# Group norm of the y tiles inside a two-direction scan: elementwise steps moved from VectorE and ScalarE to GpSimd

## The reference, cut to what matters

```python
_, ys = lax.scan(step, S0, xs)
y = (ys[:, 0] + ys[::-1, 1]).transpose(1, 0, 2, 3)       # two directions summed, (B, T, H, N)
mu = jnp.mean(y, axis=-1, keepdims=True)
var = jnp.mean(jnp.square(y - mu), axis=-1, keepdims=True)
y = ((y - mu) * lax.rsqrt(var + LNX_EPS)).reshape(B, T, C)
y = (y * lnx_g + lnx_b)                                   # then bonus, gate, output projection
```

## Time and profile before

| | value |
|---|---|
| runs | 1659.62 us median of 3 (1654.68 to 1660.95) |
| profiled execution | 1656.46 us, span 1654.7 us |
| TensorE busy in the span | 1476.4 us (89%) |
| VectorE busy | 791.2 us (48%) |
| ScalarE busy | 462.9 us (28%) |
| GpSimd busy | 46.0 us (3%) |
| mean granted TensorE clock | 0.944 |

### The profile page before, as it was taken

One profiled execution on the slowest core, in us unless ns is written; L12 is line 12 of the kernel. 1 busy time (PEld: TensorE's weight loads), 2 busy tenths in 40 slices (PEclk: granted clock), 3 DMA queues, 4 the chain that ended last, 5 costly groups with the idle time before them and its releaser, 6 DMA issues.

```text
span 1654.7 us, 27385 instructions
## 1 busy us (share of the span) xinstructions
PE 1476.4 (89%) x11156; PEld 1088.5 (66%) x11156; DVE 791.2 (48%) x985; ACT 462.9 (28%) x685; POOL 46.0 (3%) x45
## 2 busy tenths in 40 slices
PE   7889899899299998973995999999999999999993
PEld 3354544544177777762883888888788888788882
DVE  5656284678066777777237333322233321233335
ACT  3414243100034555553122333211122210122221
POOL 0100010101100000002000000000000000000000
PEclk9999999999688999886997999999999999999997
DMA  5045737463655565521110111111111111111112
GB/s 190 29 114 118 171 86 165 106 157 89 198 175 155 145 201 163 181 68 58 64 40 23 51 40 49 51 51 51 38 51 51 43 46 51 40 50 51 38 38 101
DMA packets 153463, 148.40 MB, mean 90 GB/s; under 512 B 75120, under 2 KB 130544, under 8 KB 153296
## 3 DMA queue, kind: packets, MB, share of 16 engines
q1 hardware_dynamic: 149136, 136.48, 28.7%
q0 software_dynamic: 1728, 5.64, 1.2%
q10 hardware_dynamic: 2560, 5.77, 1.1%
HBM read 106.04 MB, written 41.81 MB: 89 GB/s over the span
## 4 chain that ended last, share of the span: by engine, by line
PE 78%; DVE 12%; ACT 3%; issue 3%; DMA 2%; SPq 1%; DVEq 0%; ACTq 0%
PE banks L490 48%; PE banks L478 16%; PE banks L655 2%; PE banks L645 1%; PE banks L687 1%; PE banks L672 1%; PE banks L615 1%; PE banks L626 1%; DVE hT L1070 1%; PE banks L560 1%; PE banks L605 1%; PE banks L696 1%; PE banks L497 1%; DVE bonusT L1067 1%; DVE h_lo L1051 1%
## 5 line engine op out<-in xcount | busy, mean ns | idle before, releaser
L490 PE MATMUL banks<-h_hi,w_hi 128*128 128x512 f32 x832 | 259.3, 393 | 27.4 <-DVE h_lo L1051 14.3
L478 PE MATMUL banks<-hT,work 128*128 128x512 f32 x576 | 255.0, 603 | 18.4 <-DVE hT L1113 6.4
L490 PE MATMUL banks<-h_lo,w_hi 128*128 128x512 f32 x832 | 257.9, 391 | 0.0
L490 PE MATMUL banks<-h_hi,w_lo 128*128 128x512 f32 x832 | 257.6, 391 | 0.0
L478 PEld LDWEIGHTS banks<-hT,work 128*128 128x128 f32 x576 | 110.5, 193 | 160.0 <-issue 146.6
L490 PEld LDWEIGHTS banks<-h_hi,w_hi 128*128 128x128 f32 x832 | 156.7, 189 | 64.7 <-issue 27.9
L938 ACT ACTIVATE w_hi<-work 128x1024 fp32r<-128x1024 f32 x76 | 80.2, 1057 | 383.7 <-PE banks L490 383.7
L490 PEld LDWEIGHTS banks<-h_lo,w_hi 128*128 128x128 f32 x832 | 157.3, 189 | 33.2
L490 PEld LDWEIGHTS banks<-h_hi,w_lo 128*128 128x128 f32 x832 | 157.3, 189 | 33.0
L1341 DVE TENSOR_TENSOR xT<-xT,banks 128x1024 f32<-128x1024 f32 (+1 forms) x32 | 39.1, 1221 | 239.8 <-PE banks L490 239.8
L490 PE MATMUL banks<-g_hi,w_lo 128*128 128x512 f32 x352 | 108.4, 389 | 0.0
(11 more groups left out here) (161 smaller groups left out, 1748.1 us busy)
## 6 DMA issues: line engine op xcount, KB each, us to landing
work<-scan_d SPq DMA_DIRECT2D x32, 768.0 KB, 4.7
work<-in_w_gu SPq DMA_DIRECT2D x44, 512.0 KB, 3.5
scan_d<-work SPq DMA_DIRECT2D x16, 1024.0 KB, 6.0
work<-in_w_in SPq DMA_DIRECT2D x20, 512.0 KB, 3.9
scan_d<-work SPq DMA_DIRECT2D x32, 256.0 KB, 6.2
work<-in_w_down SPq DMA_DIRECT2D x16, 512.0 KB, 3.6
work<-v_d SPq DMA_DIRECT2D x64, 64.0 KB, 4.5
xT<-in_xT POOLq DMA_DIRECT2D x8, 512.0 KB, 7.8
```

The costliest lines, as they stand in the source:

```text
L478: mm = pe.matmul(out[:, h * HALF:(h + 1) * HALF], wt[:, k, :], src[:, k, h * HALF:(h + 1) * HALF], start=(k == 0), stop=(k == kn - 1))
L490: mm = pe.matmul(out[:, h * HALF:(h + 1) * HALF], wp[slot][:, k, :], xp[:, k, h * HALF:(h + 1) * HALF], start=(k == 0 and p_ == 0), stop=( ...
```

## The change

In the late passes, GpSimd now adds the two directions, subtracts the mean, squares (as a product of the centred tile with itself) and multiplies by the inverse deviation. VectorE keeps the sum over heads with its scaling (`y_mean`, at the places of `y_centre`), both variance sums (now both in q = 3) and the reciprocal (`y_inverse`, at the place of `y_normalise`). ScalarE keeps the square root and no longer squares in the scan. The tail's two tiles are done as before, behind a new wait for GpSimd's last product.

```diff
--- before.py
+++ after.py
@@ -921,8 +921,6 @@
 
                                 act.wait_ge(ys_stored[q % 2], 64 * (2 * i + q // 2) + FREE)
                             act.activation(Ys[q % 2][:, z], banks[:, z, 0:256], ACT.Copy).then_inc(sz[z]["Y_out"], 1)
-                        if late and q in (1, 2):
-                            y_square(2 * i + (q - 1 - 2 * YT), q - 1)
             exponentials(2 * (NC // 4) - 1, 1, (3,))
             transposed(2 * (NC // 4) - 1)
             attended(NC // 4 - 1, 1)
@@ -1035,6 +1033,28 @@
                 pool.dma_start(xT[:, k, :], a["xT"][:, k, :]).then_inc(s["x_again"], 16)
 
 
+            heads = lambda x: x.rearrange("p (h n) -> p h n", n=HD)
+            by_head = lambda x: x.rearrange("p (e j) c -> p j e c", e=2)
+            with pool.Fori(YT, NC // 4) as i:
+                for slot in range(2):
+                    r = i + (1 - YT)
+                    pool.wait_ge(y_full[slot], 16 * r)
+                    pool.tensor_tensor(ysum[slot], yin[slot][:, 0], yin[slot][:, 1], ALU.add).then_inc(yin_used[slot], 1)
+                for slot in range(2):
+                    m = 2 * i + (slot - 2 * YT)
+                    pool.wait_ge(s["y_chain"], 2 * m + 2)
+                    pool.tensor_tensor(heads(ycen[slot]), heads(ysum[slot]),
+                                       stat[slot][:, 0].unsqueeze(2).broadcast_to([P, AH, HD]), ALU.subtract)\
+                        .then_inc(s["y_cent"], 1)
+                    pool.wait_ge(s["y_cent"], m + 1)
+                    pool.tensor_tensor(ysq[slot], ycen[slot], ycen[slot], ALU.mult).then_inc(s["y_sq"], 1)
+                for slot, tile in ((0, i * -1 + NC // 4), (1, i + -1)):
+                    pool.wait_ge(s["y_inv"], 2 * i + (slot - 2 * YT) + 1)
+                    pool.tensor_tensor(yn[:, :, bass.ds(tile, 1), :].rearrange("p j o (e c) -> p j (o e) c", e=2),
+                                       by_head(heads(ycen[slot])),
+                                       by_head(stat[slot][:, 3].unsqueeze(2).broadcast_to([P, AH, HD])), ALU.mult)\
+                        .then_inc(s["y_normed"], 1)
+
             for k in range(NPAIR, KD):
                 pool.wait_ge(sp_s["att_hi"], k - NPAIR + 1)
                 pool.tensor_tensor(h_lo[:, k, :], oT[:, k, :], h_hi[:, k, :].bitcast(F32), ALU.subtract)\
@@ -1248,6 +1268,18 @@
 
             heads = lambda x: x.rearrange("p (h n) -> p h n", n=HD)
 
+            def y_mean(m, r, slot):
+
+                dve.wait_ge(yin_used[slot], r + FREE)
+                dve.tensor_reduce(stat[slot][:, 0], heads(ysum[slot]), AX.X, ALU.add).then_inc(s["y_chain"], 1)
+                dve.wait_ge(s["y_chain"], 2 * m + 1)
+                ts(stat[slot][:, 0], stat[slot][:, 0], 1.0 / HD, None, ALU.mult).then_inc(s["y_chain"], 1)
+
+            def y_inverse(m, slot):
+
+                dve.wait_ge(s["y_sd"], m + 1)
+                dve.reciprocal(stat[slot][:, 3], stat[slot][:, 2]).then_inc(s["y_inv"], 1)
+
             def y_centre(m, r, slot):
 
                 dve.wait_ge(y_full[slot], 16 * r)
@@ -1294,9 +1326,8 @@
                         if cc == 0:
                             dve.wait_ge(s["p_exp"], 8 * i + 4 * g + FREE)
                             logits(i, g, (0, 1, 2, 3))
-                        if late and q == 2:
+                        if late and q == 3:
                             y_variance(2 * i - 2 * YT, 0)
-                        elif late and q == 3:
                             y_variance(2 * i + (1 - 2 * YT), 1)
                         for z in range(2):
                             c = n if z == 0 else (i * -4 + (NC - 1 - q))
@@ -1307,12 +1338,13 @@
                             tt(S[:, z], St[:, z], PC[:, z, :, bass.ds(c, 1)].broadcast_to([P, NPAIR, HD]), ALU.mult)\
                                 .then_inc(sz[z]["S_new"], 1)
                         if late and q in (1, 2):
-                            y_centre(2 * i + (q - 1 - 2 * YT), i + (1 - YT), q - 1)
+                            y_mean(2 * i + (q - 1 - 2 * YT), i + (1 - YT), q - 1)
                         elif late and q == 3:
-                            y_normalise(2 * i - 2 * YT, i * -1 + NC // 4, 0)
-                            y_normalise(2 * i + (1 - 2 * YT), i + -1, 1)
+                            y_inverse(2 * i - 2 * YT, 0)
+                            y_inverse(2 * i + (1 - 2 * YT), 1)
 
             normalise(2 * (NC // 4) - 1, 1)
+            dve.wait_ge(s["y_normed"], NT - 2 + FREE)
             for slot in range(2):
                 y_centre(NT - 2 + slot, NT // 2, slot)
             for slot in range(2):
```

## The result

The changed kernel takes 1649.96 us, the one before 1658.83 us beside it (medians of 14 runs each). The ratio is 0.9948, 95% interval 0.9929 to 0.9967: 8.9 us faster, and clear of no change. The forecast was 1651.3 us, 8.3 us less.

What follows compares the result with a forecast made beforehand. TensorE holds 78% of the chain of waits, so VectorE savings count only where TensorE waits. Savings of 1.23 + 1.53 = 2.76 us in each of three late passes make 8.3: 1659.62 - 8.3 = 1651.3 us, range 1645 to 1660.

Steps and rivals of the forecast that it cites:

- q = 3: Late pass, end of q = 2 to TensorE's next L645: ScalarE no longer squares, saving 1.53 us.
- The bound: TensorE holds 78% of the chain; group norm's 18 us in three late passes are all the change can touch in the scan.
- q = 2: Late pass, between the ends of VectorE's last state products: 9.71 us instead of 10.94, saving 1.23 us.
- the two products: End of q = 3, the two L1273 moved to GpSimd: beside TensorE's wait for the Y copies, so worth nothing.
- g, GpSimd's instruction: Duration of one GpSimd instruction on a 128x512 tile: taken as 1.09 us, kept between 1.0 and 2.16.
- the slower rival: Long GpSimd instructions delay VectorE in q = 2 and q = 3: with 2.16 us each, 1664.2 us; chance 0.15.
- The add's cover: End of q = 1: GpSimd's add is over by about 674.5, `y_mean` comes at 676.2, 1.7 us in hand.
- if L1307 is stretched in q = 1: Sign that the prediction would be wrong: VectorE's state product in q = 1 takes longer; no size given.
- The clock rival: TensorE's clock in q = 0 moves: 3 us less, 1648.3, or as much more, 1654.3; chance 0.1 each.

Runs made afterwards that it cites:

- square twice: The changed kernel with each square done twice on GpSimd, first into a spare tile: 1650.20 us, ratio 0.9944.
- the held-back one: The changed kernel with GpSimd's subtraction and square of slot 0 held back until VectorE's L1266 of q = 2 is done: 1647.03 us, ratio 0.9926.

## Why the prediction was right

- **The bound.** That only the scan's late passes could gain, and there only q = 2 and q = 3, holds: 8.65 us of the profile lie there. Putting back what was costed at nothing (the two products) changed nothing; putting back what was costed (the squares) did.
- **g, GpSimd's instruction.** Taken 1.09 us, measured 1.04 for subtraction and square, 1.06 for the product and 1.27 for the add. The broadcast operand, which gave the slower rival its case, costs nothing: the subtraction has one, the square none.
- **q = 2.** Forecast 9.71, measured 9.21, so 1.73 us saved instead of 1.23. The order is the one forecast (L1262 slips in or waits, the square goes first, L1266 waits for it), with L1266 at 2.47 against "about 2.6". Its terms were a little long, all four in the same direction: the hand-over from VectorE to GpSimd, 0.08 us instead of 0.23; that between GpSimd's two instructions, 0.08 instead of 0.2; the two instructions themselves, 0.10 together; and the start of VectorE's product, of which some 0.15 us pass while it waits (L1266 ends 1.62 us after the square, and takes 1.76 where nothing is in its way).
- **q = 3.** Forecast 8.24, measured 8.18, 1.59 us saved instead of 1.53. L1252 was stretched by 0.08 instead of 0.4, within the slack. Both variance sums end in time. The edit with the squares on ScalarE shows that 1.27 us of this saving are ScalarE's. That holds for passes 5 and 6. The third pass has no L645 behind it; from the end of its q = 2 to the tail's first add it took 24.91 us before and 23.32 after, which is 1.59 less as well, but 23.32 with the squares back on ScalarE too, and 21.89 with the subtraction held back. Whether q = 3 earned the third 1.59 isn't shown.
- **The add's cover.** `y_mean` doesn't wait for it, as forecast. But the prediction looked only at that wait and missed the other side: in pass 5, the y load lands later and the add runs into the first state product, 1.18 us instead of 0.43. q = 1 takes 8.05 instead of 7.30. It had named "if L1307 is stretched in q = 1" as what would make it wrong, and this step of it was, by 0.75 us once. These two rows are VectorE's and GpSimd's of the changed kernel:

```profile
647.87 1.18 DVE L1338 TENSOR_TENSOR work<-work,PC 128x256 f32<-128x256 f32 x1
```

```profile
646.16 2.60 POOL L1042 TENSOR_TENSOR work<-work 128x512 f32<-128x512 f32 x2 [189.28 <-DMA work<-y_d]
```

- **The slower rival.** Its mechanism holds for a longer instruction, but its price was too high: "4 us a pass for each us of g". With the square alone longer by 0.85 us, half of that rule is 1.7; the pass grew by 0.85 + 0.42 = 1.27, as q = 3 has more slack than was counted. In the changed kernel ScalarE starts its exponentials 0.49 us after the negated maxima are there (pass 6), where the prediction had the maxima 0.06 us late.
- **The clock rival** is real but goes both ways: q = 0 took 12.03 and 9.10 us in the changed kernel, 10.49 and 10.48 before, the sum nearly the same.

The sum therefore closes: three times 1.73 + 1.59 is 9.96, minus 0.75 for pass 5; the remaining difference to 8.65 is q = 0 and q = 1 of the single passes (1.54 and 0.41 lost, 1.38 gained). That the total came so near to the forecast 8.3 is in part luck. The two places gave 1.7 us more than forecast, and q = 1, at which nothing was forecast, took 1.16 back. And the clock moved single q = 0 pieces by 1.5 us between these two kernels and by up to 4.4 between all, so a forecast that is right to 0.6 us is closer than its mechanism can vouch for.

## What to carry to other kernels

An engine that is 28% busy can be the one that holds up the step: look for what its next instruction waits for, not for its load. When elementwise work goes to GpSimd, find VectorE's products with two SBUF inputs (and its small operations of one input, like the negated maxima) and keep GpSimd's reads away from them by one wait, or at least keep GpSimd's instructions short: in these traces VectorE got in between two of them and never into one that reads. And before hiding a table switch in a loop, ask whether the function can be applied once, behind the loop.

## What the runs showed of the hardware that was not expected

- Between two GpSimd instructions 0.08 us apart, a waiting VectorE product takes its turn, and then the second GpSimd instruction waits for all of it (2.44 us instead of 1.04).
- A small VectorE instruction with one SBUF input (negated maxima, 128x4) was held up by GpSimd's square, 0.95 us instead of 0.17.
- The clock can do more to a late pass than the edits: its q = 0 spreads over 4.4 us, and q = 2 and q = 3 gained 3.3 together. TensorE waits about 1.35 us for the Y copies, and the matmuls behind that wait often run at the lower level. Windows of the changed kernel, q = 0 after passes 5 and 6:

```profile
668.00:676.00 8.00, 8.00 (x114) 5.49 (x112) 5.58 (x11) 2.81 (x7) 1.37 (x2) 0.58 0.74 204
704.00:712.00 8.00, 7.80 (x197) 6.18 (x192) 6.18 (x13) 3.81 (x9) 1.68 (x2) 1.00 0.69 210
```

  In one it was granted 0.58 of full clock (1.2 GHz most of the time), in the other 1.00 (2.4 GHz), and the piece took 12.03 and 9.10 us. Of the 18 such pieces in the nine profiles that keep the root ahead of the Y copies, three took 9.10, the others 10.46 to 13.55; their mean is 11.6 us. The piece follows the clock. Windows of 8 us from 0.5 us behind the piece's L645 show 0.50 of full clock where it took 13.5 (square twice, after pass 6, first row), 0.79 where it took 10.49 (the kernel before, both), and 1.00 where it took 9.10. With the roots out of the scan TensorE doesn't wait there, was granted 1.00 both times (second row), and both pieces took 9.29:

```profile
691.10:699.10 8.00, 8.00 (x98) 5.58 (x94) 4.17 (x8) 2.92 (x7) 1.50 (x2) 0.50 0.69 202
```

```profile
684.60:692.60 8.00, 7.57 (x185) 5.97 (x185) 6.36 (x13) 2.98 (x10) 2.07 (x2) 1.00 0.65 179
```

  Two such pieces at 2.3 us below the mean are 4.6 us. With the 3.6 us of shorter work that makes 8.2 of the 12.0 us which that kernel gained over the held-back one; the other 3.8 are not accounted for, and are within the intervals of the two ratios. That the wait brings the clock down is the likeliest reading, but it isn't shown: no run changed the wait and nothing else, and the three pieces of 9.10 had a wait of 1.35 to 1.65 us in front of them as well, and kept the full clock.
